# Rotary embedding by copied partner rows instead of permutation products, in a three-layer decoder on one core

## What is computed

```python
def rms_norm(x, g, eps=RMS_EPS):
    xf = x.astype(jnp.float32)
    y = xf * lax.rsqrt(jnp.mean(xf * xf, axis=-1, keepdims=True) + eps)
    return (y * g.astype(jnp.float32)).astype(x.dtype)

def apply_partial_rope(t, cos, sin):        # diffk, diffq: 16 of 64 columns
    half = ROT_DIM // 2
    tf = t.astype(jnp.float32)
    r1 = tf[..., :half]
    r2 = tf[..., half:ROT_DIM]
    c = cos[:, :, None, None, :]
    s = sin[:, :, None, None, :]
    out = jnp.concatenate([r1 * c - r2 * s, r1 * s + r2 * c, tf[..., ROT_DIM:]], axis=-1)
    return out.astype(t.dtype)

def rope(x, pos):                           # win: all 64 columns
    ...
    x1, x2 = xf[..., :half], xf[..., half:]
    return jnp.concatenate([x1 * cos - x2 * sin, x2 * cos + x1 * sin], axis=-1).astype(x.dtype)
```

## Time and profile before

| | |
|---|---|
| median of 3 runs | 1307.94 us (1307.29 to 1310.09) |
| the profiled execution | 1307.87 us |
| its span | 1306.1 us |
| TensorE, share of the span | 92% |
| VectorE | 70% |
| ScalarE | 46% |
| GpSimd | 8% |
| granted TensorE clock, mean | 0.96 of full |

### The profile page before, as it was taken

One profiled execution on the slowest core, in us unless ns is written; L12 is line 12 of the kernel. 1 busy time (PEld: TensorE's weight loads), 2 busy tenths in 40 slices (PEclk: granted clock), 3 DMA queues, 4 the chain that ended last, 5 costly groups with the idle time before them and its releaser, 6 DMA issues.

```text
span 1306.1 us, 24112 instructions
## 1 busy us (share of the span) xinstructions
PE 1206.7 (92%) x9138; PEld 1137.4 (87%) x9138; DVE 918.1 (70%) x1514; ACT 597.7 (46%) x1012; POOL 106.8 (8%) x82
## 2 busy tenths in 40 slices
PE   5999999999999999989999999989968796899995
PEld 5988898999999999679899999989945586899995
DVE  7997776766665786656767666558876358899855
ACT  5653644544444422444444444442265343556541
POOL 1585110100000000001010000110000001000000
PEclk9999999999999999999999999998977687899998
DMA  7454352445455544134435555544440021455551
GB/s 254 173 184 139 102 189 97 162 161 192 168 186 194 194 162 161 40 123 148 143 101 190 193 170 184 183 176 158 148 175 1 1 97 65 139 183 193 184 203 65
DMA packets 30825, 195.29 MB, mean 150 GB/s; under 512 B 3232, under 2 KB 7456, under 8 KB 7712
## 3 DMA queue, kind: packets, MB, share of 16 engines
q1 hardware_dynamic: 30752, 194.27, 42.6%
HBM read 193.21 MB, written 1.05 MB: 149 GB/s over the span
## 4 chain that ended last, share of the span: by engine, by line
PE 76%; DVE 14%; ACT 4%; issue 3%; DMA 1%; ACTq 0%; DVEq 0%; SPq 0%
PE acc L465 20%; PE acc L467 19%; PE acc L466 19%; PE acc L499 5%; DVE wlo L1231 2%; PE acc L481 2%; DVE wlo L1224 2%; PE acc L761 2%; ACT whi L887 2%; DMA raw<-weights 1%; PE sc L725 1%; PE sc L532 1%; PE tp L465 1%; PE tp L467 1%; PE tp L466 1%
## 5 line engine op out<-in xcount | busy, mean ns | idle before, releaser
L465 PE MATMUL acc<-Hhi,whi 128*128 128x256 f32 x1376 | 395.9, 288 | 12.4 <-DVE wlo L1231 12.4
L466 PE MATMUL acc<-Hlo,whi 128*128 128x256 f32 x1376 | 391.4, 284 | 0.0
L467 PE MATMUL acc<-Hhi,wlo 128*128 128x256 f32 x1376 | 391.2, 284 | 0.0
L887 ACT ACTIVATE whi<-raw 128x1024 fp32r<-128x1024 f32 x163 | 172.2, 1056 | 406.8 <-PE acc L467 384.3
L1224 DVE TENSOR_TENSOR wlo<-raw,whi 128x1024 fp32r<-128x1024 f32 x164 | 205.7, 1254 | 113.8 <-ACT whi L887 111.7
L465 PEld LDWEIGHTS acc<-Hhi,whi 128*128 128x128 f32 x1376 | 266.2, 193 | 16.5 <-DVE wlo L1231 14.7
L466 PEld LDWEIGHTS acc<-Hlo,whi 128*128 128x128 f32 x1376 | 266.2, 193 | 1.6 <-issue 1.4
L467 PEld LDWEIGHTS acc<-Hhi,wlo 128*128 128x128 f32 x1376 | 266.1, 193 | 0.0
L465 PE MATMUL acc<-FH,whi 128*128 128x256 f32 x848 | 240.2, 283 | 15.7 <-DVE wlo L1231 9.3
L467 PE MATMUL acc<-FH,wlo 128*128 128x256 f32 x848 | 239.0, 282 | 0.0
L1231 DVE TENSOR_TENSOR wlo<-raw,whi 128x1024 fp32r<-128x1024 f32 x164 | 204.2, 1245 | 1.3
(11 more groups left out here) (262 smaller groups left out, 1784.1 us busy)
## 6 DMA issues: line engine op xcount, KB each, us to landing
raw<-weights SPq DMA_DIRECT2D x177, 1024.0 KB, 4.9
MEM<-mem_in SPq DMA_DIRECT2D x2, 1024.0 KB, 10.9
held<-weights SPq DMA_DIRECT2D x2, 1024.0 KB, 6.2
cst<-consts SPq DMA_DIRECT2D x1, 1126.0 KB, 11.5
X<-x_in SPq DMA_DIRECT2D x4, 256.0 KB, 3.6
raw<-weights SPq DMA_DIRECT2D x2, 512.0 KB, 6.8
out<-X SPq DMA_DIRECT2D x4, 256.0 KB, 2.1
PT<-positions SPq DMA_DIRECT2D x1, 128.0 KB, 12.2
```

Source lines behind the costliest of these rows:

```text
L465: pe.matmul(dst, w, x, start=first, stop=False)
L466: pe.matmul(dst, w, xl, start=False, stop=False)
L467: return pe.matmul(dst, wl, x, start=False, stop=last)
L887: act.activation(whi[j][:, 0:HALF, :], raw[j][:, 0:HALF, :], ACT.Copy).then_inc(hi_out, 1)
```

## The change

The permutation matrices and their fifteen products go. The columns of the weights (and the matching constants) are reordered on the host so that a row and its partner lie on neighbouring partitions: in diff partitions 0 and 1 of every 8, in win every even and odd one. The sine's sign is folded into its table.

ScalarE copies each rotated tile out of PSUM as it is, without the norm's factor (`as_it_is`), which frees the accumulator. Then it makes the weight step of tile k+2, and then issues two DMAs which swap the partners from `A` into `E` (`partners`): 16 rows each in diff, 64 rows each in win, 2 KB a row. `E` has three slots, and a slot's next use waits for the rotation that read it. GpSimd zeroes `E` once, behind the squares of `ffn0`.

VectorE makes two tables from cosine and sine times `R` (`tables`), once for diff and once for win, and a rotation is three operations on SBUF which wait for the partners. The evacuation of the rotated tiles on VectorE is gone.

In win the weight steps of tiles 3 and 4 move into the norm. The function `ahead` is passed in as `between`: the first behind the root of `final`, the second behind the second step of the root of `pre2`. In diff the weight step of tile 3 stands behind the norm and the tables. The loops over these stages are written out.

```diff
+            def as_it_is(name, k):
+                at = ROT_SLOT[name] + 2 * k
+                act.wait_ge(tile_done, T0[name] + k + 1)
+                src = first_acc if k == 0 and name != "diffq" else acc[k % 2][:, :, :]
+                act.activation(A[:, at:at + 2, :], src, ACT.Copy).then_inc(acc_free, 1)
+
+            def partners(name, k):
+                n, at, every = ROT0[name] + k, ROT_SLOT[name] + 2 * k, APART[name]
+                act.wait_ge(acc_free, G0[name] + k + 3)
+                if n == 0:
+                    act.wait_ge(turned_zero, 1)
+                if n >= 3:
+                    act.wait_ge(rot_used, n - 2)
+                for half in range(2):
+                    act.dma_start(E[half::every, n % 3, :, :], A[1 - half::every, at:at + 2, :]).then_inc(partner_in[n % 3], 16)
...
-                pe.matmul(sc[:, n % 2, :], perm, pairs, start=True, stop=True).then_inc(rot_ready, 1)
...
+            def rotate(name, k):
+                n, at = ROT0[name] + k, ROT_SLOT[name] + 2 * k
+                q, partner = A[:, at:at + 2, :], E[:, n % 3, :, :]
+                dve.wait_ge(partner_in[n % 3], 2 * 16 * (n // 3 + 1))
+                link(dve.tensor_tensor(out=q, in0=q, in1=both(cos_r), op=ALU.mult))
+                link(dve.tensor_tensor(out=partner, in0=partner, in1=both(sin_r), op=ALU.mult))
+                dve.tensor_tensor(out=q, in0=q, in1=partner, op=ALU.add).then_inc(rot_used, 1)
...
                 link(inverse_root("final", S, D, eps, RF))
+                between[0]()
                 link(dve.tensor_tensor(out=R[:, :], in0=RF, in1=RF, op=ALU.mult))
-                link(inverse_root("pre2", S, D, eps, R[:, :], times=R[:, :]))
+                link(inverse_root("pre2", S, D, eps, R[:, :], times=R[:, :], between=between[1]))
...
-            project("win", A, "pre2")
+            ahead("win", 0, 8, 0)
+            norm("pre2", [lambda: ahead("win", 0, 8, 1), lambda: ahead("win", 0, 8, 2)])
+            tables("win")
+            for k in range(3):
+                rotate("win", k)
+            for k in range(3, 7):
+                projected("win", k)
...
+                if name == "ffn0":
+                    pool.memset(E[:, :, :, :], 0.0).then_inc(turned_zero, 1)
```

More of the change, by code:

```diff
@@ L273, in build @@
         ROT_SLOT = {"diffk": 8, "diffq": 0, "win": 0}
+        APART = {"diffk": 8, "diffq": 8, "win": 2}
         KC_SLOT, Q_SLOT, KS_SLOT, KW_SLOT, KSW_SLOT, VC_SLOT = 0, 2, 10, 11, 12, 14
@@ L945, in plain @@
                 turns = NTILES[name] // 2
[L946 to L949, removed]
+                for i in range(turns):
+                    for j in range(2):
+                        rotated = 2 * i + j < ROTS.get(name, 0)
+                        if rotated:
+                            as_it_is(name, 2 * i + j)
+                        ahead(name, i, 2, j)
+                        if rotated:
+                            partners(name, 2 * i + j)
+            def as_it_is(name, k):
[12 more added lines that the diff above has]
+                    act.dma_start(E[half::every, n % 3, :, :], A[1 - half::every, at:at + 2, :]).then_inc(partner_in[n % 3], 16)
             def late_keys(k):
@@ L1283, in inverse_root, with norm @@
                         link(ins)
+                    if step == 1 and between:
+                        between()
                 return ins
             NORM_LINKS = 2 + 3 * 3
-            def norm(name, eps=RMS_EPS):
+            def norm(name, between=None, eps=RMS_EPS):
                 if name != "pre2":
@@ new lines, in tables, with projected, project @@
+            def tables(name):
+                for dst, src in ((cos_r, "cos2"), (sin_r, "sin2")):
+                    table = C(src) if name == "win" else rope_c[:, :] if src == "cos2" else rope_s[:, :]
+                    link(dve.tensor_tensor(out=dst, in0=table, in1=R[:, :], op=ALU.mult))
+            def projected(name, k):
+                ahead(name, 0, NTILES[name], k)
+                rotate(name, k)
+            def project(name, dst, norm_name=None):
+                turns = first_turn(NTILES[name] // 2, norm_name)
@@ L1731, in _ @@
                 residual("down0", 6, [(Hhi, Hlo, "g_kv"), (H2hi, H2lo, "g_mix1")])
-                project("diffk", A[:, 8:16, :], "attn1")
-                project("diffq", A[:, 0:8, :], before="diffk")
-                values("diffv", lambda i, j, tt: slot(MKV, 4 * i + (2 * DC + 2 * j + tt)), "attn1", "diffq")
+                ahead("diffk", 0, 4, 0)
+                norm("attn1")
+                tables("diffk")
+                ahead("diffk", 0, 4, 1)
+                rotate("diffk", 0)
+                rotate("diffk", 1)
+                projected("diffk", 2)
+                projected("diffk", 3)
+                for k in range(4):
+                    projected("diffq", k)
+                dve.wait_ge(acc_free, G0["diffv"] + 2)
+                values("diffv", lambda i, j, tt: slot(MKV, 4 * i + (2 * DC + 2 * j + tt)), "attn1")
                 attention("attn_diff")
@@ L1847, in _, with in_heads @@
                 add_normed(x_final)(p)
+TURNED1 = [d + 8 * half for d in range(8) for half in range(2)]
+_rest = iter(range(ROT1, HD2))
+TURNED1 = [TURNED1[p // 8 * 2 + p % 8] if p % 8 < 2 else next(_rest) for p in range(HD2)]
+TURNED2 = [d + 32 * half for d in range(32) for half in range(2)]
+def in_heads(order, a, n=MB):
+    return [c + d for c in range(a, a + n, HD2) for d in order]
 def column_tile(w, cols, k0=0):
```

110 lines of the change are left out of this document (35 added, 75 removed).

## The result

| | before | changed | ratio, 95% interval |
|---|---|---|---|
| first comparison (4 runs each) | 1307.62 us | 1297.89 us (1296.3 to 1303.29) | 0.9936 (0.9916 to 0.9956) |
| second comparison (22 and 12 runs) | 1307.55 us | 1299.81 us (1295.86 to 1304.72) | 0.9955 (0.9938 to 0.9971) |
| all runs of the comparisons (48 and 16), median | 1307.30 us | 1299.72 us | |
| the same, mean | 1306.85 us | 1300.17 us | |

The change makes the kernel faster, by 0.45 to 0.64%: 6.7 us by the means of all runs, where 4.8 were forecast. The profiled execution of the changed kernel was its slowest of those runs, 1303.29 us for a span of 1301.5, so its span must not be held against the 1306.1 of before. It is read by sections instead.

A forecast was written before the change was run, and what follows sets the result against it. The prediction took TensorE to bound the kernel in the rotated stages. A gain of 5.85 us in diff and a loss of 1.0 in win gave -4.8 us, from 1307.87 to 1303.1 us; range 1300.0 to 1307.0.

The forecast's parts named there:

- The product's price and what bounds the kernel: In diffk, diffq and win TensorE sets the pace; each rotation product costs it 0.85 us, fifteen cost 12.8 us.
- Steady state: Between the heads and ends of the stages, the wait for partners is covered: 9.7 us needed, 11.5 us available.
- landing: Partner transfers in diff and win land 2.2 us after issue, range to 3.6; up to 3.9 us costs nothing.
- small edits: Zeroing E, fewer constant columns and unrolled loops cost nothing, at worst 0.6 us for the zeroing.
- The head of diffk: TensorE idles 0.35 us ahead of tile 3 and 0.6 ahead of tile 4; diff section gains 5.85 us.
- The head of win: VectorE stands 6.7 us for ScalarE's half; TensorE stands 5.2 us ahead of tile 5, which pays 1.9 for the clock.
- the rival without a fall: In win, the clock does not fall behind TensorE's 5.2 us wait: 1301.1 us, chance 0.18.
- The rival of the whole gain: VectorE is not late in win, so all fifteen products go for nothing: 1295.1 us, chance 0.07.
- The end of win: Partner issue follows copy and halves; last rotation ends at 935.4, block pieces start after 938.2; win section loses 1.0 us.
- a term put at nothing: Behind win's block pieces, the rest of the chain moves as a block, with no gain or loss of its own.
- The sum: Whole kernel: -5.85 us in diff and +1.0 in win give -4.8 us, from 1307.87 to 1303.1 us.
- The range: Whole kernel: 1300.0 to 1307.0 us, covering the forecast, no clock fall and serial transfers, leaving 0.15 out.

The follow-up runs named there:

- experiment 6: Changed kernel with win's weight steps of tiles 3 and 4 behind norm and tables, diffk's ahead of tables and rotation 1; 1292.67 us, ratio 0.9889.
- experiment 4: Changed kernel without the thirty partner transfers, so partners stay zero and the rotation is wrong; 1301.15 us, ratio 0.9959.
- experiment 7: Changed kernel with partners moved for all rows in diff, 64 rows a transfer in place of 16; 1297.64 us, ratio 0.9923.
- experiment 2: Changed kernel with win's weight steps of tiles 3 and 4 put behind the norm and the tables; 1295.13 us, ratio 0.9917.
- experiment 9: Changed kernel with win's weight steps kept inside the roots, but its rotations spread between later tiles' weight steps; 1293.9 us, ratio 0.9905.
- experiment 5: Changed kernel with one more wait on ScalarE, so partner DMAs are issued only after both weight halves; 1299.8 us, ratio 0.9949.

## Why the prediction was right, and where not

The prediction failed at one step that the runs show, the time of the partner issue at the end of win, and in the width of its range, which held no scatter of the kernel's own time. The rest of the mechanism held. About 1 us of the first result stays unplaced.

**The product's price and what bounds the kernel: right.** 5.76 us a tile without it, and experiment 6, with nothing late, gains 6.80 us for eight products.

**Steady state, landing, small edits: right.** The transfers are covered (experiments 4 and 7); VectorE waits for them twice in the first profile of the changed kernel, 1.9 us in all, the longest here:

```profile
473.69 0.69 DVE L1377 TENSOR_TENSOR A<-A,nw 128x512 f32<-128x512 f32 x1 [1.59 <-DMA E<-A]
```

and this falls in time that VectorE had free. The Trainium skill ("DMA: Bandwidth & Descriptors", "Rules for kernel authors") speaks against two transfers to disjoint partition halves since they serialize. Whatever they do to each other, here it lies in cover: leaving them out changes neither section of the change by more than 0.1 us.

**The head of diffk: right.** 0.95 us forecast in two waits (0.35 and 0.6), 0.35 and 0.70 found, and experiment 6 gets 1.06 back. Differential section -5.85 forecast, -5.74 measured.

**The head of win: right to 0.5 us.** With the 2.24 us added by which this execution is earlier: VectorE's wait ends at 893.3 (893.8 forecast), tile 5's halves end at 913.8 (914.3), TensorE waits 5.02 (5.2), the clock falls behind it (the rival without a fall is out, though its 1301.1 us is near the result). The fall cost more than forecast. The raw copies of tiles 4 and 5 start 13.15 us apart (906.68 and 919.83); less the wait and a tile of 5.76, that leaves 2.4 us for the 1.9 of the forecast. With the half us by which tile 5 starts early, its end comes out at 922.1 as forecast, so two errors of half a us cancel.

```profile
919.83 0.60 ACT L938 ACTIVATE A<-acc 128x512 f32<-128x512 f32 x1 [10.66 <-PE acc L472]
```

The 0.53 of 882 to 889, from which the prediction read "half of it" at 1.2 GHz, means nearly all of that stretch: full speed throughout is 1.00 and 1.2 GHz throughout is 0.50. The 1.9 us came from the products' spacing and do not rest on this. Experiments 2 and 9 show that the order is the cause, and which part of it: with the wait kept and the three rotations spread, 5.4 of the 6.5 us come back. The rival of the whole gain is what experiments 2 and 6 build.

**The end of win: the step that failed.** "From the end of tile 6: copy and halves to 930.7, issue and landing to 933.3". I read ScalarE's program order as the order in which things happen and put the issue behind the halves. The trace shows it at 926.22 + 2.24 = 928.5, ahead of the second half. The last rotation so starts at 931.7 in place of 933.3, and the block pieces:

```profile
934.77 2.55 DVE L1801 TENSOR_TENSOR A<-A,cst 64x120 f32<-64x120 f32 x8
```

at 937.0 for the 938.2 forecast and 937.16 in the earlier trace rows. Win comes out at -0.15 us for +1.0 (by the means of two profiles each, -0.05). Experiment 5 builds the forecast's order and finds 0.8 to 0.9 of the 1.2. The rest is about what the head of win was early by, which is an argument and not a run.

**Cmp: a term put at nothing.** I moved everything behind the block pieces as a block. Cmp takes 22.1 us for 22.65 and 23.20, so 0.5 to 1.1 less, 0.8 by the means of two profiles each. TensorE's wait ahead of cmp's second tile went from 3.29 us to

```profile
948.55 0.30 PE L470 MATMUL acc<-whi,FH 128*30 128x256 f32 x1 [2.20 <-DVE wlo L1231]
```

and the clock in 948 to 955 is 0.93 for the 0.52 of 951 to 957. But the next wait went the other way, first before, then changed:

```profile
957.00 0.28 PE L465 MATMUL acc<-whi,FH 128*30 128x256 f32 x1 [0.78 <-DVE wlo L1231]
```

```profile
954.66 0.39 PE L470 MATMUL acc<-whi,FH 128*30 128x256 f32 x1 [3.15 <-DVE wlo L1231]
```

So the two waits together are longer in the changed kernel, 5.35 us for 4.07, and what became shorter is the time at the low clock: behind the two waits it stands at 0.52 and 1.00 before (951 to 957, 957 to 963), at 0.93 and 0.75 in the changed kernel (948 to 955, 954.5 to 960.5). Over all twelve profiles neither wait orders the section: experiment 5 has 3.05 and 1.73 us and takes 22.14, experiment 2 has 2.79 and 3.15 and takes 23.16, and the four profiles of the kernel before and its variants take 23.20, 22.65, 23.18 and 22.46. That the change gained the 0.8 us in cmp is therefore not shown; it may be the clock's scatter, and the cause stays open.

**The sum.** By the means of two profiles each, -5.74 - 0.05 - 0.8 = -6.6 us for the -4.8 forecast. The means over all runs differ by 6.7. The two agree, but the agreement is in part luck: sections that the change does not touch move by up to 4 us between profiles, and the spans of the same four profiles differ by 5.45. Of the 5.2 us between the forecast, 1303.1, and the first result, 1297.89, the end of win is 1.05 (shown), cmp 0.8 (not shown to come from the change), and 0.6 is that the forecast started from one execution of 1307.87 us where the median of all is 1307.3.

**The range.** Another 1.8 us, 1297.89 against 1299.72 over all sixteen runs, are the kernel's own spread, and the last 1 us has no place. I built the range from the bounds of the unknown costs and left the scatter of a small sample out, though a stretch of 350 us that the change does not touch varies by 4 us. With 2 us of scatter the lower end would have been 1298, and the result would still have lain 0.1 below it.

## What to carry to other kernels

Removing a product pays its full price only where the engine that feeds the next tile is not made late; here 0.85 us a product where it held, and nothing for seven products where a weight step had been moved to stand between two roots. When a step that waits is put early on an in-order engine, count what stands in a row between it and the next step that the bounding engine needs: the wait of 6.5 us cost 1.1 us of the section with the rotations spread (experiment 9 against 2), and 6.5 with three of them in a row behind it. Judge such a change by its sections between common events, since the whole spreads over 9 us and the two sections that hold the change repeat to 0.1 to 0.3. Sections further on do not: from the last gelu to the first tap of the last up projection, which no edit touches, the twelve profiles take 134.4 to 141.0 us.

## What the hardware showed that was not expected

- **An issue overtakes.** ScalarE's queue sent out a DMA that stands behind two activations in program order 0.8 us before the second of them started (926.22 against 927.03). Nothing in the trace shows it waiting for them, and experiment 5, which adds a wait, moves it. "What stands behind a waiting instruction waits too", as written ahead of the prediction, holds for VectorE's 6.55 us wait; it says nothing of a DMA behind activations that are only running. A DMA that must come later needs a wait of its own, and one whose data is ready costs its engine's activations nothing visible: the halves stand 0.95 us apart with the issue (926.08, 927.03) and without one between (922.50, 923.45).
- **Landing is not set by size alone.** 32 KB took 2.8 us, 128 KB 2.1 in the same execution. By the straight line of the Trainium skill ("DMA: Bandwidth & Descriptors", "Anatomy of one DMA"), fitted there to transfers issued by GpSimd where these are ScalarE's, 32 KB would be an estimated 2.1; the measurement decides. (The prediction's estimate of 2.3 us for 128 KB goes by the same line; 2.1 were measured.) The median of the 128 KB transfers went from 2.1 to 3.7 us between kernels that differ only in VectorE's order, and issued 2 us later (experiment 5) the small ones took 1.9. What else is in flight is the likely reason; it was not measured.
- **The clock behind a wait goes by more than the wait's length.** In win, TensorE's waits of 5.02 and 4.96 us were followed by 0.50 and 0.56, the one of 0.92 us by 1.00. In cmp it is not so plain: 3.29 us were followed by 0.52 and 2.20 us by 0.93, and behind the 3.15 us wait the clock stood at 0.75:

```profile
954.50:960.50 6.00, 5.84 (x40) 5.06 (x41) 2.59 (x4) 3.60 (x5) 0.00 (x0) 0.75 0.78 287
```

Waits of about 3 us were thus followed by different clocks, and cmp, where no edit changed an instruction, took 22.1 to 23.2 us over the twelve profiles.
